# A hand-written order of the scan's operations on four engines, written anew, with operations from one or two turns back

## The reference

```python
    G = jnp.cumsum(g, axis=-1)
    gamma = jnp.exp(jnp.where(incl, G[..., :, None] - G[..., None, :], -jnp.inf))
    kb = k * beta[..., None]
    a_low = jnp.where(strict, jnp.einsum('bhnid,bhnjd->bhnij', kb, k) * gamma, 0.0)
    ...
    uw = lax.linalg.triangular_solve(eye + a_low, rhs, left_side=True, lower=True, unit_diagonal=True)
    ...
    def step(s, inp):
        u_n, w_n, qk_n, qd_n, kd_n, gl_n = inp
        v_new = u_n - jnp.einsum('bhck,bhkv->bhcv', w_n, s)
        o_n = jnp.einsum('bhck,bhkv->bhcv', qd_n, s) + jnp.einsum('bhij,bhjv->bhiv', qk_n, v_new)
        s = s * jnp.exp(gl_n)[..., None, None] + jnp.einsum('bhck,bhcv->bhkv', kd_n, v_new)
        return s, o_n
```

## Time and profile before

| | us |
|---|---|
| median of three runs | 3566.6 (3563.71 to 3573.29) |
| the profiled execution's own time | 3574.62 |
| its span in the profile | 3572.8 |
| TensorE's matmuls busy in the span | 3451.9 |
| VectorE busy in the span | 2172.1 |
| first matmul of the scan of half 0 | 1580.51 |
| its last matmul's end | 1788.28 |

### The profile page before, as it was taken

The page is one execution under the profiler, slowest core; times in us unless marked ns, Lnnn a source line. Parts: engine busy times, 40 slices in busy tenths (PEclk is TensorE's granted clock), DMA queues, the critical chain, the costliest instruction groups (busy, mean ns, idle before and its releaser), DMA issues.

```text
span 3572.8 us, 59170 instructions
## 1 busy us (share of the span) xinstructions
PE 3451.9 (97%) x24990; PEld 2877.7 (81%) x24990; DVE 2172.1 (61%) x3040; ACT 980.9 (27%) x1835; POOL 473.9 (13%) x400
## 2 busy tenths in 40 slices
PE   8999999999999999999999999999999999999998
PEld 6777887877778888879887887799988786668887
DVE  4655777646557776655565556854475653864347
ACT  1243101222430012433343322443322203720011
POOL 0000000000000000015402440034440001502000
PEclk9999999999999999999999999999999999999999
DMA  4311444323015443210010013032252331022222
GB/s 173 111 37 48 185 189 176 137 100 112 25 50 207 188 166 125 104 37 3 3 65 25 3 48 125 36 114 100 106 194 71 104 116 48 1 72 104 95 95 95
DMA packets 58055, 338.93 MB, mean 95 GB/s; under 512 B 7580, under 2 KB 8092, under 8 KB 23240
## 3 DMA queue, kind: packets, MB, share of 16 engines
q1 hardware_dynamic: 30492, 220.50, 16.9%
q10 hardware_dynamic: 27308, 114.71, 8.8%
HBM read 309.64 MB, written 18.21 MB: 92 GB/s over the span
## 4 chain that ended last, share of the span: by engine, by line
PE 76%; DVE 8%; PEld 6%; DMA 3%; issue 3%; ACT 2%; PEldq 1%; POOL 0%; POOLq 0%; ACTq 0%; DVEq 0%; another core or an unknown queue 0%; SPq 0%
PE psum L567 19%; PE psum L569 18%; PE psum L568 18%; PE psum L2650 4%; PE psum L2657 4%; DMA pieces_in<-pieces 2%; PEld psum L567 2%; PEld psum L569 2%; PEld psum L568 2%; PE psum L1412 1%; PE psum L1396 1%; PE psum L1385 1%; PE psum L2789 1%; PEldq L507 1%; PE psum L4234 1%
## 5 line engine op out<-in xcount | busy, mean ns | idle before, releaser
L569 PE MATMUL psum<-xt_operands,pieces_lo 128*128 128x512 f32 (+1 forms) x2016 | 748.9, 371 | 0.0
L567 PE MATMUL psum<-xt_operands,pieces_hi 128*128 128x512 f32 (+1 forms) x1840 | 700.2, 381 | 16.3 <-DVE xt_operands L826 7.0
L568 PE MATMUL psum<-xt_operands,pieces_hi 128*128 128x512 f32 (+1 forms) x1840 | 689.7, 375 | 0.0
L567 PE MATMUL psum<-pieces_hi,xt_operands 128*128 128x512 f32 x1276 | 508.9, 399 | 18.5 <-DVE pieces_lo L616 9.4
L568 PE MATMUL psum<-pieces_lo,xt_operands 128*128 128x512 f32 x1320 | 517.6, 392 | 0.0
L569 PE MATMUL psum<-pieces_hi,xt_operands 128*128 128x512 f32 x1276 | 500.6, 392 | 0.0
L569 PEld LDWEIGHTS psum<-xt_operands,pieces_lo 128*128 128x128 f32 x2016 | 379.6, 188 | 62.7
L567 PEld LDWEIGHTS psum<-xt_operands,pieces_hi 128*128 128x128 f32 x1840 | 346.9, 189 | 87.6 <-issue 13.6
L568 PEld LDWEIGHTS psum<-xt_operands,pieces_hi 128*128 128x128 f32 x1840 | 347.2, 189 | 59.2
L583 DVE CAST pieces_hi<-pieces_in 128x2048 fp32r<-128x2048 f32 x165 | 208.2, 1262 | 254.5 <-DMA pieces_in<-pieces 125.2
L567 PEld LDWEIGHTS psum<-pieces_hi,xt_operands 128*128 128x128 f32 x1276 | 242.3, 190 | 76.4 <-DVE pieces_lo L616 10.5
(11 more groups left out here) (464 smaller groups left out, 5586.6 us busy)
## 6 DMA issues: line engine op xcount, KB each, us to landing
pieces_in<-pieces SPq DMA_DIRECT2D x210, 1024.0 KB, 4.9
x_mem<-ada ACTq DMA_DIRECT2D x28, 1024.0 KB, 4.8
arena<-ada ACTq DMA_DIRECT2D x20, 1024.0 KB, 4.8
hid<-arena ACTq DMA_DIRECT2D x22, 384.0 KB, 4.4
arena<-mods ACTq DMA_DIRECT2D x10, 512.0 KB, 17.0
arena<-hid ACTq DMA_DIRECT2D x3, 1536.0 KB, 11.6
...
```

The lines of the kernel that those rows point to most:

```text
L567: signal_later(k, pe.matmul(out, sh, mh, start=start, stop=False, skip_group_check=reopened))
L568: signal_later(k, pe.matmul(out, sh, ml, start=False, stop=False, skip_group_check=reopened))
L569: return pe.matmul(out, sl, mh, start=False, stop=stop, skip_group_check=reopened)
```

## The change

The table of orders is a new one for all four engines. On TensorE operations of like shape now stand more often beside each other, and the turn begins elsewhere; two marks `''` mean two turns back. The number of operations is the same. `LAG` is the largest distance in turns, and the loops run so many turns longer to finish. Since the old order made many waits needless (another wait or the place in the queue covered them), the operations now name all that they need: what they read, and what must have read the buffer that they write. `seen` still leaves out what is covered.

```diff
 ORDERS = {
-    "pe": order("a3.0' x4.0' a1.1' x8.0' ks.1' wy.0' x2.1' a2.1' qk.1' xx0.0' a3.1' z0.0' x4.1' y1.0' o1.1' x8.1' "
...
+    "pe": order("a3.1'' x4.1'' wy.0'' x8.1'' gb.1' xx0.0'' wy.1'' z0.0'' y1.0'' xx0.1'' z0.1'' ks.1'' y1.1'' xx1.0'' "
...
+LAG = max(back for ops in ORDERS.values() for _, _, back in ops)
...
-        for turn in range(steps + 1):
+        for turn in range(steps + LAG):
...
+CORNERS = [key[1:] for _, key in sorted(PE_AT.items()) if key[0] == "xx2"]
+CORNER_AHEAD = dict(zip(CORNERS[1:], CORNERS))
...
         for need in needs:
-            back = need.startswith("-")
+            back = len(need) - len(need.lstrip("-"))
             self.seen(need.lstrip("-"), s - back, d)
...
+        if name in ("ks", "o1") and s == 0:
+            pe.wait_ge(k.S.padding_ready, 2 + d)
...
     def z0(s, d):
         if not runs(s):
             return
-        ready(s, d, "z0", ())
+        ready(s, d, "z0", ("wya",))
...
     def l2c(s, d):
-        copy2(s, d, "l2c", "l2", "a1", "a1")
+        copy2(s, d, "l2c", "l2", "a1", "a1", "-a2", "-x2")
...
     def xf(s, d):
         if runs(s):
-            st.begin("xf", s, d, ("xx0",))
+            st.begin("xf", s, d, ("xx0", "--vn", "--w2", "--y2", "--y1"))
...
     def half_copy(s, d, name, src, *needs):
         if runs(s):
             rows, _ = halves(d)
+            if (s, d) in CORNER_AHEAD:
+                st.seen("xx2", *CORNER_AHEAD[s, d])
             st.begin(name, s, d, needs)
...
     for d in range(2):
-        e.link(dve.memset(k.state[d], 0.0))
+        dve.memset(k.state[d], 0.0).then_inc(k.S.padding_ready, 1)
...
     def bv(s, d):
-        tt(s, d, "bv", k.buf[d]["rr"], chunk(k.vc_, s, d), col(BETA, s, d), ALU.mult)
+        tt(s, d, "bv", k.buf[d]["rr"], chunk(k.vc_, s, d), col(BETA, s, d), ALU.mult, "-vn")
...
     def s1(s, d):
-        tt(s, d, "s1", k.state[d], k.state[d], col(ETOT, s, d), ALU.mult, "o1")
+        tt(s, d, "s1", k.state[d], k.state[d], col(ETOT, s, d), ALU.mult, "o1", "ks", "-s2")
```

More of the change, by code:

```diff
@@ L2501 @@
 ORDERS = {
-    "pe": order("a3.0' x4.0' a1.1' x8.0' ks.1' wy.0' x2.1' a2.1' qk.1' xx0.0' a3.1' z0.0' x4.1' y1.0' o1.1' x8.1' "
[L2503 to L2509, removed]
+    "pe": order("a3.1'' x4.1'' wy.0'' x8.1'' gb.1' xx0.0'' wy.1'' z0.0'' y1.0'' xx0.1'' z0.1'' ks.1'' y1.1'' xx1.0'' "
+      "qk.1'' xx1.1'' w2.0'' y2.0'' w2.1'' y2.1'' xx2.0'' o1.1'' xx2.1'' vn.0'' o1.0'' o2.0'' kk.0' vn.1'' "
+      "su.0'' o2.1'' kk.1' qk.0' ul.0' gb.0 ks.0' su.1'' a1.0' ul.1' x2.0' a2.0' a1.1' a3.0' x4.0' a2.1' "
+      "x2.1' x8.0' "),
+    "dve": order("wya.1'' r1.1'' qg.1'' rr.1'' rr.0'' v2a.0'' v2a.1'' t1.1'' t1.0'' t2.0'' s2.0'' low0.0' low.0' "
+      "t2.1'' ulm.0' low0.1' low.1' lvm.0' qg.0' s2.1'' diff.0 ulm.1' r1.0' lvm.1' x2a.0' x4a.0' x2a.1' "
+      "x8a.0' x4a.1' wya.0' x8a.1' diff.1 "),
+    "act": order("z0c.0' z0c.1' y1c.1' v1c.0' v1c.1' w2c.0' y2c.0' y2c.1' w2c.1' vnc.0' vnc.1' gamt.0 gam.0 gam.1 "
+      "gamt.1 l2c.0 l4c.0 l2c.1 l8c.0 l4c.1 l8c.1 xf.0 xf.1 y1c.0 "),
+    "pool": order("dup.0 dlow.0 dup.1 dlow.1 x1.0 s1.1' oa.0' bv.1 x1.1 kd.0 kd.1 oa.1' bv.0 s1.0 "),
 }
+LAG = max(back for ops in ORDERS.values() for _, _, back in ops)
 def counted(steps):
@@ L2739, in wy @@
             return
-        ready(s, d, "wy", ("x8a",))
+        ready(s, d, "wy", ("x8a", "lvm"))
         out = small2(k, "wy", s, d)
@@ L2813, in o2 @@
     def o2(s, d):
-        product(s, d, "o2", b("qg"), b("vn"), "vnc")
+        product(s, d, "o2", b("qg"), b("vn"), "qg", "vnc")
     def su(s, d):
[L2817 to L2826, removed]
+        product(s, d, "su", b("kd"), b("vn"), "kd", "vnc")
+    for t in range(N_STEPS + LAG):
+        a3(t - 2, 1); x4(t - 2, 1); wy(t - 2, 0); x8(t - 2, 1); gb(t - 1, 1); xx0(t - 2, 0); wy(t - 2, 1)
+        z0(t - 2, 0); y1(t - 2, 0); xx0(t - 2, 1); z0(t - 2, 1); ks(t - 2, 1); y1(t - 2, 1); xx1(t - 2, 0)
+        qk(t - 2, 1); xx1(t - 2, 1); w2(t - 2, 0); y2(t - 2, 0); w2(t - 2, 1); y2(t - 2, 1); xx2(t - 2, 0)
+        o1(t - 2, 1); xx2(t - 2, 1); vn(t - 2, 0); o1(t - 2, 0); o2(t - 2, 0); kk(t - 1, 0); vn(t - 2, 1)
+        su(t - 2, 0); o2(t - 2, 1); kk(t - 1, 1); qk(t - 1, 0); ul(t - 1, 0); gb(t, 0); ks(t - 1, 0); su(t -
+        2, 1); a1(t - 1, 0); ul(t - 1, 1); x2(t - 1, 0); a2(t - 1, 0); a1(t - 1, 1); a3(t - 1, 0); x4(t - 1,
+        0); a2(t - 1, 1); x2(t - 1, 1); x8(t - 1, 0)
 def scan_act(k, e, _):
@@ L2884, in v1c @@
         if runs(s):
-            st.begin("v1c", s, d, ("xx1",))
+            st.begin("v1c", s, d, ("xx1", "xf"))
             for rows, others in quarters(d):
@@ L2944, in diff @@
     def diff(s, d):
-        tt(s, d, "diff", k.buf[d]["t"], ps("gb", s, d), col(PRE, s, d), ALU.subtract, "gb")
+        tt(s, d, "diff", k.buf[d]["t"], ps("gb", s, d), col(PRE, s, d), ALU.subtract, "gb", "-low", "-dup")
     def low0(s, d):
@@ L3009, in s2 @@
         tt(s, d, "s2", k.state[d], ps("su", s, d), k.state[d], ALU.add, "s1", "su")
-    for t in range(N_STEPS + 1):
-        diff(t, 0); wya(t - 1, 1); diff(t, 1); v2a(t - 1, 0); v2a(t - 1, 1); t1(t - 1, 0); t2(t - 1, 0)
-        s2(t - 1, 0); low0(t, 0); low(t, 0); qg(t, 0); ulm(t, 0); t2(t - 1, 1); low0(t, 1); lvm(t, 0); low(t, 1)
-        s2(t - 1, 1); r1(t, 0); x2a(t, 0); ulm(t, 1); x4a(t, 0); rr(t, 0); x8a(t, 0); lvm(t, 1); wya(t, 0)
-        r1(t, 1); rr(t, 1); x2a(t, 1); qg(t, 1); x4a(t, 1); x8a(t, 1); t1(t, 1)
+    for t in range(N_STEPS + LAG):
+        wya(t - 2, 1); r1(t - 2, 1); qg(t - 2, 1); rr(t - 2, 1); rr(t - 2, 0); v2a(t - 2, 0); v2a(t - 2, 1)
+        t1(t - 2, 1); t1(t - 2, 0); t2(t - 2, 0); s2(t - 2, 0); low0(t - 1, 0); low(t - 1, 0); t2(t - 2, 1)
+        ulm(t - 1, 0); low0(t - 1, 1); low(t - 1, 1); lvm(t - 1, 0); qg(t - 1, 0); s2(t - 2, 1); diff(t, 0)
+        ulm(t - 1, 1); r1(t - 1, 0); lvm(t - 1, 1); x2a(t - 1, 0); x4a(t - 1, 0); x2a(t - 1, 1); x8a(t - 1,
+        0); x4a(t - 1, 1); wya(t - 1, 0); x8a(t - 1, 1); diff(t, 1)
 def scan_pool(k, e, _):
@@ L3038, in dlow @@
         t = k.buf[d]["t"]
-        tt(s, d, "dlow", t, t, heads(gmask[:, d, :]), ALU.add, "dup")
+        tt(s, d, "dlow", t, t, heads(gmask[:, d, :]), ALU.add, "diff", "dup")
     def dup(s, d):
@@ L3061, in oa @@
             tt(s, d, "oa", o, o, k.buf[d]["tb"], ALU.add, "t2")
[L3063 to L3065 removed]
+    for t in range(N_STEPS + LAG):
+        dup(t, 0); dlow(t, 0); dup(t, 1); dlow(t, 1); x1(t, 0); s1(t - 1, 1); oa(t - 1, 0); bv(t, 1); x1(t,
+        1); kd(t, 0); kd(t, 1); oa(t - 1, 1); bv(t, 0); s1(t, 0)
 def head_norm_act(k, e, mix, nt, sq):
```

51 lines of the change are left out of this document (24 added, 27 removed).

## The result

The changed kernel took 3627.01 us (median of four runs, 3613.32 to 3634.22) against 3568.27 (3563.71 to 3573.29) for the kernel before on the same chip: a ratio of 1.016, 95% interval 1.0126 to 1.0193. It is slower by some 59 us; forecast were 23 us less. The profiled execution took 3626.1 us. (Two slow executions of a later kernel, e8, of 8696.2 and 7825.2 us, are left out of its median and ratio.)

What follows compares the result with a forecast made beforehand. TensorE was taken to bound the scan. A half gains 14.0 + 0.8 - 1.0 - 1.2 - 1.0 - 0.35 = 11.25 us, both 22.5, say 23, from the median 3566.6 to 3543 us; range 3534 to 3554.

Steps and rivals of the forecast that it cites:

- The joins: TensorE in the scan: fewer changes of matmul shape, 182 to 90 a half, save 14.0 us a half.
- The nine 128x128 operations from vn.0 to qk.0: Sign in the profile after: these TensorE operations stand in one stretch of about 8.2 us.
- the ends of the halves: End of each scan: o2.1's wait goes, gaining 0.8 us; wy.1 waits for x8a.1, losing 0.35.
- The waits: Tight places in the scan where TensorE would wait: losses of 1.0, 1.2, 1.0 and 0.35 us a half.
- ul.0 waits 0.26 us for low.0: Scan turn: low.0 meets GpSimd's dup.1, so ul.0 waits 0.25 us, five times, 1.2 a half.
- The waits of xx0.1 and a1.1: In the scan, xx0.1 waits 0.16 us for wya.1, a1.1 some 0.2 for ulm.1; 1.0 a half each.
- Likeliest, small waits: Main case for the whole kernel: joins less small waits in the scan give 3543 us, chance 0.64.
- the six 32x32 operations from xx0.0 to z0.1: Sign in the profile after: this run on TensorE takes 2.0 us.
- a wait that I walked past in one of the in-order queues: Named as what above all would make the forecast wrong: an overlooked wait, repeated ten times; no size given.
- The clock: Low granted clock at a half's head: put at nothing; 4.5 us a half lost if low one stretch longer.
- the one that ended slower: Rival: GpSimd's queue in written order delays low.0's chain beyond TensorE's cover; over 10.7 us slower, chance 0.03.
- the bad meetings: Rival: low.0 also meets dlow.1 and low.1 always meets s1.1 in scan turns; 3551 us, chance 0.18.

Runs made afterwards that it cites:

- e8: e2 with one more wait per turn, among the 128x128 operations (kk.1 also waits for dup.1): 3555.4 us.
- e2: The changed kernel with half as many 32x32 matmuls in wy, xx0 and z0, each over twice the columns: 3537.90 us.
- e3: The old order with half as many 32x32 matmuls in wy, xx0 and z0, each over twice the columns: 3561.30 us.
- e11: The kernel before, with wy.0 of one chunk in each half issuing its 64 matmuls sixteen times: 3632.21 us.
- e5: e2 with one more wait per turn, behind the 32x32 operations (w2.0 also waits for rr.0): 3605.50 us.
- e6: e2 with two 128x128 operations moved on TensorE, ks.1 ahead of gb.1 and qk.1 behind wy.1: 3591.61 us.

## Why the prediction was wrong, by its steps

*The joins* (14.0 us a half) were right as far as the runs show. e2 and e3 differ by 23.4 us where the whole sum, joins less waits, gave 22.5. The nine 128x128 operations from vn.0 to qk.0 were to take 8.2 us; in the changed kernel they start at 1682.46 and ul.0 at 1691.14, 8.68 us with the 0.26 of its wait and some 0.2 of the last result. The split was off: a steady turn gains 1.6 (32.45 to 30.83), not 1.9, though waits that were counted in didn't come up, and the ends of the halves gain more. That the totals lie so close is in part luck.

*The waits* were right in one place. ul.0 waits 0.26 us for low.0, with 0.25 forecast, and low.0 takes 1.32. The rule of the Trainium skill, "SBUF — State Buffer", "Who interferes with whom" (whoever issues first holds the shared ports and the other blocks fully), would have low.0 end 0.69 us after dup.1; the trace again has 0.55. The waits of xx0.1 and a1.1 (1.0 a half each) didn't come up: a steady turn of e2, where no supply hides them, has 0.34 us of idle in all, 0.26 of it ahead of ul.0.

*The step that failed* is that each operation was priced by its own duration alone: "Likeliest, small waits", with 2.0 us for the six 32x32 operations from xx0.0 to z0.1. They took 1594.84 to 1599.39 in the first turn, 4.55 us, because instructions come at 127 matmuls in 3.3 to 3.9 us while these operations use 127 in 1.1 us. The ten operations of 32x32 in a turn are 320 matmuls or 2.5 packets, at least 8 us of supply (2.5 times 3.3), and the new order gave them little else to stand among. The prediction looked for what else could end late in queues and ports, and walked past a queue of DMA with a load of 1%. Its own last sentence, "a wait that I walked past in one of the in-order queues", has the kind right, but it was looked for among the engines.

A rule of the Trainium skill leads the same way astray: "Runtime: NRT & Kernel Launch", "Instruction fetch mechanics", says that the sequencer fetches 16 KiB blocks of 256 instructions ahead and that the cost of crossing one is mostly hidden. The block's size agrees with the trace (packets of 16 KB, 128 matmuls and as many weight loads in each); that it is hidden doesn't hold for small matmuls, where a crossing costs up to 2.24 us (2.73 in e11).

*The clock* was put at nothing, with 4.5 us a half if one more stretch stayed low. By subtraction it is the larger part of the loss. Of the 56.2 us in the scans 27.7 are idle; the new order takes some 23 away (e2 against e3); so some 52 come from the 125 us more at 1.2 GHz. (As an estimate from two rows: 125 us in which 2.08 us of work would take 1.16 lose 55, and in which 0.60 would take 0.41 lose 40.) e5 against e2 shows that idle next to small operations brings the clock down when a wait for data ends it, not only late instructions. Supply is the first cause, since e2, with fewer instructions in the same order, has hardly any idle and no fall in its steady turns.

*The rivals.* Neither the one that ended slower (GpSimd's queue in its written order) nor the bad meetings took place. The range had no mechanism in it by which TensorE's own speed could change.

*Open.* The round of 3.3 us and more is seen in its parts (a packet takes 0.9 to 1.5 of it), but not why the next packet starts only after the matmuls have gone on, nor what the time between its landing and the matmuls is spent on. Nor is it shown how much idle among small operations the clock bears: two turns of half 0 had interruptions of up to 1.57 us and kept it. And whether the four short waits of e6 would bring it down without its longer run of small operations was not tried.
